# Tile 1's gates moved from the first stage into the gathers, routing at turns 1, 3, 5 and 8, and the first unit's norm, scores and route taken in parts

## The reference, cut to what matters

```python
h = modulate(rms_norm(x, g_mix), sh1, sc1)
q_sb, k_sb, v_sb, q_d, k_d, v_d, gate_sb, gate_d = split(h @ w_in)
merged = sigmoid(gate_sb) * br_sb + sigmoid(gate_d) * br_d
x  = x + gt1 * (merged @ w_out)
h2 = modulate(rms_norm(x, g_ffn), sh2, sc2)
# peer_ffn: for each token and each of 8 heads
q   = h2 @ w_pq                       # two halves of 128
sub = q . keys                        # 2 x 128 scores
s_top, i_top = top_k(sub, 16)         # of each half
best, pos = top_k(s_top[0][:, None] + s_top[1][None, :], 16)
expert = (i_top[0] * 128 + i_top[1])[pos]          # 16 rows per token and head
act = gelu(h2 . peer_u[expert])
out = sum(softmax(best) * act * peer_v[expert])
```

## Time and profile before

| what | value |
|---|---|
| median of 3 runs | 1521.73 us (1521.61 to 1535.05) |
| the profiled execution's own time | 1517.63 us |
| its span | 1515.8 us |
| PE, DVE, ACT, POOL busy | 1319.8, 725.9, 303.8, 557.4 us |
| mean DMA rate | 335 GB/s, 507.33 MB in packets |
| first gather issued | 277.88 us |
| first dots of units 0, 1, 4 and 8 | 282.20, 319.6, 457.67, 665.1 us |

### The profile page before, as it was taken

The page is one execution under the profiler, slowest core; times in us unless marked ns, Lnnn a source line. Parts: engine busy times, 40 slices in busy tenths (PEclk is TensorE's granted clock), DMA queues, the critical chain, the costliest instruction groups (busy, mean ns, idle before and its releaser), DMA issues.

```text
span 1515.8 us, 13732 instructions
## 1 busy us (share of the span) xinstructions
PE 1319.8 (87%) x4628; PEld 746.7 (49%) x4628; DVE 725.9 (48%) x1642; ACT 303.8 (20%) x735; POOL 557.4 (37%) x531
## 2 busy tenths in 40 slices
PE   7999999568779796695798999888898998999997
PEld 7767788434445463342443444343333343554443
DVE  5125333787676566665566575664534322320001
ACT  2221112332211112211221321111110122411102
POOL 1000000477776666676565554645554000000000
PEclk6999999779999898897899999999999999999999
DMA  8945544789999999999999999999999789678882
GB/s 352 399 181 208 205 157 139 259 308 389 385 377 385 409 393 404 409 400 360 370 382 410 409 409 409 409 409 409 409 409 408 276 305 412 225 251 278 286 302 90
DMA packets 135284, 507.33 MB, mean 335 GB/s; under 512 B 15408, under 2 KB 16304, under 8 KB 133168
## 3 DMA queue, kind: packets, MB, share of 16 engines
q0 software_dynamic: 75456, 293.63, 49.4%
q1 hardware_dynamic: 58320, 208.63, 37.5%
q10 hardware_dynamic: 1440, 4.19, 0.7%
HBM read 505.35 MB, written 1.05 MB: 334 GB/s over the span
## 4 chain that ended last, share of the span: by engine, by line
PE 54%; DMA 23%; DVE 8%; another core or an unknown queue 5%; issue 5%; POOL 2%; ACT 2%; SPq 0%; DVEq 0%; ACTq 0%
PE ps_M L844 19%; DMA arena<-in_peer_u,arena 18%; PE ps_M L400 8%; PE ps_T L646 7%; PE ps_T L647 6%; DMA ring<-in_w_second 3%; DVE tmp L1879 3%; PE ps_M L621 2%; PE ps_M L592 2%; PE ps_M L410 2%; DMA ring<-in_peer_v,arena 2%; POOL ring L1113 1%; PE ps_S L421 1%; POOL arena L1100 1%
## 5 line engine op out<-in xcount | busy, mean ns | idle before, releaser
L844 PE MATMUL ps_M<-ring,arena 128*128 128x512 f32 x1088 | 498.5, 601 | 13.1 <-DMA ring<-in_w_second 9.5
L1100 POOL DMA_INDIRECT arena<-in_peer_u,arena x256 | 273.1, 1067 | 267.7 <-DVE tmp L1879 120.8
L1113 POOL DMA_INDIRECT ring<-in_peer_v,arena x256 | 277.1, 1082 | 166.1 <-issue 66.8
L646 PE MATMUL ps_T<-ring,arena 128*128 128x512 f32 x436 | 240.5, 635 | 105.9 <-ACT arena L1251 40.7
L844 PEld LDWEIGHTS ps_M<-ring,arena 128*128 128x128 f32 x1088 | 203.7, 193 | 252.5 <-issue 241.1
L647 PE MATMUL ps_T<-ring,arena 128*128 128x512 f32 x436 | 235.0, 622 | 0.0
L1879 DVE SCALAR_TENSOR_TENSOR tmp<-arena,merged 128x1024 f32<-128x1024 f32 x128 | 156.7, 1224 | 160.6 <-DMA arena<-in_peer_u,arena 135.5
L1879 DVE SCALAR_TENSOR_TENSOR tmp<-arena 128x1024 f32<-128x1024 f32 x128 | 156.6, 1224 | 74.9 <-DMA arena<-in_peer_u,arena 65.9
L646 PEld LDWEIGHTS ps_T<-ring,arena 128*128 128x128 f32 x436 | 77.5, 198 | 200.8 <-issue 143.9
L647 PEld LDWEIGHTS ps_T<-ring,arena 128*128 128x128 f32 x436 | 87.2, 200 | 112.0 <-issue 112.0
L400 PE MATMUL ps_M<-hT,ring 128*128 128x256 f32 x576 | 130.3, 386 | 1.3 <-ACT hT L1264 1.3
(11 more groups left out here) (257 smaller groups left out, 1075.7 us busy)
## 6 DMA issues: line engine op xcount, KB each, us to landing
ring<-in_w_second SPq DMA_DIRECT2D x276, 512.0 KB, 4.5
arena<-in_w_ada POOLq DMA_DIRECT2D x12, 2048.0 KB, 11.0
ring<-in_w_in SPq DMA_DIRECT2D x46, 512.0 KB, 11.4
ring<-in_w_pq SPq DMA_DIRECT2D x32, 512.0 KB
ring<-in_w_out SPq DMA_DIRECT2D x16, 512.0 KB, 4.2
ring<-in_w_br SPq DMA_DIRECT2D x16, 384.0 KB, 3.0
arena<-in_peer_u,arena POOLq DMA_INDIRECT x256
ring<-in_peer_v,arena POOLq DMA_INDIRECT x256
```

The lines of the kernel that those rows point to most:

```text
L646: low = mm(twin[:, 0:512], dg[:, i % 8, :], v_ring[n % VR][:, 0:512], start=first, stop=last)
L844: m = mm(bank, left[c], w[:, c, :], start=first and c == 0, stop=last and c == 1)
L1100: pool.indirect_dma_start(u_ring[:, n % UR, :], None, A["peer_u"][0], bass.IndirectOffsetOnAxis(ap=expert[:, u % 3, k:k + 1], axis=0))\
L1113: pool.indirect_dma_start(v_ring[n % VR], None, A["peer_v"][0], bass.IndirectOffsetOnAxis(ap=expert[:, u % 3, k:k + 1], axis=0))\
```

## The change

Six edits, all in the order of the programs:

1. The gates of tile 1 leave the first stage. `tile_gate(0, ...)` computes tile 0's with 128 moving columns; tile 1's are 16 products `lga`, `lgb`, four in each of phases -1, 0, 1 and 2, at turns 1, 4, 9 and 12 on TensorE and one turn later on ScalarE. SP loads their weights a second time, in `FIRST` between the queries.
2. The route of a unit is at turns 1, 3, 5 and 8 of its phase, where it was at 2, 5, 8 and 11.
3. The sum of squares of unit 0's norm is taken in parts between the products of `out1`.
4. Unit 0's scores are two products in two banks, each behind its own query half, and each half is copied and routed by itself.
5. `stick_scores1(0)`, `stick_old(0)` and `stick_mask1(0)` come later: behind the row transposes on TensorE, behind the row copies on ScalarE, behind unit 0's route on VectorE.
6. `merge` waits for the gate's Tanh by a semaphore of its own.

```diff
+def late_gates(phase):
+    return [(("lga", "lgb")[n % 2], n // 2) for n in range(4 * (phase + 1), 4 * (phase + 2))]
...
+    elif phase < 3:
+        FIRST += late_gates(phase)[:2] + [(f"q{u}", 0), (f"q{u}", 1)] + late_gates(phase)[2:]
...
+            def tile_gate(t, name):
+                bank = claim_m(name)
+                w = tile(name)
+                for c in range(KC):
+                    m = mm(bank[:, 0:P], w[:, c, :], hT[:, c, tile_tok(t)], start=c == 0, stop=c == KC - 1)
+                finish(m, name)
...
+            def norm_part(c):
+                pe.wait_ge(sq_ready, KC + c + 1)
+                m = mm(ps["SA"][:, 0:P], ones[:, :], squares[:, c, :], start=c == 0, stop=c == KC - 1)
+                if c == KC - 1:
+                    finish(m, ("norm2", 0))
...
+            def half_scores(half):
+                name = ("sub", 0, half)
+                bank = claim(("OT", "T0")[half], name)
+                pe.wait_ge(*emptied(("q0", half)))
+                finish(mm(bank[:, 0:NK], qT[:, half, :], keysT[:, half, :], start=True, stop=True), name)
...
-                both_tiles(("ga", c))
-                both_tiles(("gb", c))
+                tile_gate(0, ("ga", c))
+                tile_gate(0, ("gb", c))
...
-            stick_scores1(0)
             for k in range(KC):
                 out1(0, k)
-            tile_norm("SA", ("norm2", 0), 1)
+                if k == 1:
+                    claim("SA", ("norm2", 0))
+                if k > 0:
+                    norm_part(k - 1)
+            norm_part(KC - 1)
             for half in range(2):
                 query(0, half)
-            scores(0)
+                half_scores(half)
             for half in range(2):
                 turn_rows(0, half, f"T{half}")
+            stick_scores1(0)
...
+                if phase < 3 and k in (1, 4, 9, 12):
+                    tile_gate(1, late_gates(phase)[(1, 4, 9, 12).index(k)])
...
-            score_take(0)
+                copy(("sub", 0, half), sub[:, 0, half, :], NK)
...
+                if phase < 3 and k in (2, 5, 10, 13):
+                    name = late_gates(phase)[(2, 5, 10, 13).index(k)]
+                    gate_tile(1, ("lga", "lgb").index(name[0]), name[1], name)
...
+                dve.wait_ge(*emptied((("gb", "lgb")[t], c)))
...
-                    if k in (2, 5):
-                        route_half(u, (k - 2) // 3)
+                    if k in (1, 3):
+                        route_half(u, k // 3)
+                    elif k == 5:
+                        route_best(u)
                     elif k == 8:
-                        route_best(u)
-                    elif k == 11:
                         route_index(u)
```

More of the change, by code:

```diff
@@ L1023, in source @@
                     return w_in_v[:, 24 + n, :]
-                if what in ("ga", "gb"):
-                    return w_in_v[:, 30 + KC * ("ga", "gb").index(what) + n, :]
+                if what[-2:] in ("ga", "gb"):
+                    return w_in_v[:, 30 + KC * ("ga", "gb").index(what[-2:]) + n, :]
                 if what in ("br0", "br1"):
@@ L1251, in diagonal, with gate_tile @@
                 F(dg[:, i % 8, :], ident[:, :], ACT.Copy, scale=wgt[:, u % 2, k:k + 1]).then_inc(diag_ready, 1)
+            def gate_tile(t, s, c, name):
+                act.wait_ge(*produced(name))
+                F(gate[:, t * KC + c, s, :], ps[use[name][0]][:, 0:P], ACT.Tanh, scale=0.5).then_inc(released(name), 1)
             act.wait_ge(vec_in, 16)
@@ L1305, in _ @@
                 for s, name in enumerate((("ga", c), ("gb", c))):
-                    act.wait_ge(*produced(name))
-                    F(gate[:, c:c + KC + 1:KC, s, :], ps[use[name][0]][:, 0:T].rearrange("p (t n) -> p t n", n=P),
-                      ACT.Tanh, scale=0.5).then_inc(released(name), 1)
+                    gate_tile(0, s, c, name)
                 if c == 1:
@@ L1318, in _ @@
                     dil_take(0, 1)
-            stick_old(0)
             F(warm[:, 1:2], eps, ACT.Sqrt)
@@ L1327, in _ @@
                 query_take(0, half)
-            score_take(0)
+                copy(("sub", 0, half), sub[:, 0, half, :], NK)
             for half in range(2):
                 copy(("rows", 0, half), h_rows[0][:, half * 512:(half + 1) * 512], 512)
+            stick_old(0)
             for half in range(2):
@@ L1828, in route_half @@
             def route_half(u, half):
-                if half == 0:
+                if u == 0:
+                    dve.wait_ge(*emptied(("sub", 0, half)))
+                elif half == 0:
                     dve.wait_ge(*emptied(("sub", u)))
@@ L1961, in _ @@
                 merge(0, c)
-            stick_mask1(0)
             own()
@@ L1970, in _ @@
             route_index(0)
+            stick_mask1(0)
             def beside(phase, k):
```

## The result

Over 19 runs of each the changed kernel has a median of 1511.64 us (1498.87 to 1519.12) and the kernel before 1525.21 us (1517.95 to 1535.05): ratio 0.990, 95% interval 0.988 to 0.992. In the rounds of the experiments, where both kernels are faster (before near 1502 us), the changed kernel stood at 0.9933, interval 0.991 to 0.995. The forecast was 1504.6 against 1521.7, 0.989, with a range of 1494 to 1519: a step of 17.1 us, where 13.6 were measured here and 10.3 in the rounds of the experiments.

The account below looks back on a forecast made before the run. TensorE was taken to bound the first stage and DMA bytes at 409 GB/s the gather stage. First gather 26.1 us earlier, gather stage 9.0 us longer: -17.1 us, giving 1504.6 us, range 1494 to 1519.

Parts of the forecast that it names:

- Three stages, the second bound by its bytes: Whole kernel: TensorE bounds the first stage, DMA bytes at 409 GB/s the gather stage; the last moves unchanged.
- Gates, 23.8 us: First stage: 16 gate tiles each lose 1.70 us, 27.2 together, less 3.4 lost waiting for a modulation chunk.
- The wait for chunk 9: TensorE in the first stage's gates: waits 4.4 us for this modulation chunk instead of 0.97, losing 3.4 us of gain.
- Chunk 11 and the ring's loads: First stage's modulation and weight loads: in time, the chunk with 0.4 us of room; if late, 5 to 8 us less gain.
- Attention scores 2.0, norm -0.9: Before the first gather: scores leave TensorE's path, gaining 2.0 us; unit 0's norm in parts loses 0.9.
- Scores and route, 1.2: Unit 0 before the first gather: scoring and routing each half by itself gains 1.2 us.
- The bytes, 20.5 less 8.5 less 3: Gather stage: second load costs 20.5 us at 409 GB/s; unit 0's room returns 8.5, units 1 to 3 return 3.
- Earlier indices, 2 us and the 1.4 MB of rows in unit 0, 3.4 us: Gather stage: POOL waits less for route indices, gaining 2 us later and bringing 1.4 MB of rows forward in unit 0.
- TensorE's lag, 2 us: Gather stage, phases 0 to 2: added gate products delay rows and ScalarE, costing 2 us, bounds 0 and 8.
- The slower rival: Phases 0 to 2: TensorE becomes the bound at the halved clock, +22.9 us, 1545; chance 0.05.
- The rival of bytes paid in full: Gather stage: the second load gets no free room, so -5.6 us in all, 1516; band 1511 to 1525, chance 0.28.
- the one in which the room takes nearly all: Gather stage: units 0 to 3 fill to 409 GB/s and index waits vanish, -26 us, 1496; chance 0.12.

Follow-up runs that it names:

- no_second_load: The changed kernel without the second load of the 16 gate tiles, tile 1's gates computed with the keys as weights; 0.9839 of the kernel before, median 1477.01 us.
- one_product: The changed kernel with only the first of the eight products of each of tile 1's gate tiles, all loads kept; 0.9941 of the kernel before.
- busy_wait: The changed kernel with one gate tile's eight products issued three times over, filling TensorE's wait for modulation chunk 9; 0.9932 of the kernel before.
- changed_again: The changed kernel unaltered, run again on one chip with the kernel before for a second trace; 0.9933 of the kernel before, median 1492.14 us.
- gates_only: The kernel before with only the move of tile 1's gates beside the gathers (edits to gates and merge's semaphore); 0.9934 of the kernel before.
- route_only: The kernel before with only the route of a unit moved to turns 1, 3, 5 and 8; 0.9994 of the kernel before.
- chunk9_later: The changed kernel with TensorE's sums of modulation chunk 9 one column tile later, behind the gates of c = 3; 0.9921 of the kernel before.

## Why the prediction was right, point by point

- **Three stages, the second bound by its bytes.** Right, and more strictly than the prediction used it: with a granted clock of 0.96 to 0.99 the stage is its bytes over 409 GB/s plus what room unit 0 leaves. Taking bytes away won 15.1 us (no_second_load), taking products away nothing (one_product). Of the Trainium skill's page "DMA: Bandwidth & Descriptors", the rule that loads from all queues share one set of DMA engines ("Issuing engines are not separate DMA queues") is borne out here, by SP's tiles that cost the rows 15.1 us; the figure of 358 GB/s ("Where 436 GB/s comes from") is not, the stage runs at 409.
- **Gates, 23.8 us.** 62.5 us became 40.7 to 41.8: 20.7 to 21.8. The wait for chunk 9 was 4.20 us, where 4.4 were predicted. Not in the sum was what it does to the clock, 3.4 to 6.8 us at the lower level, worth 1.6 us by busy_wait; with the clock whole the gates take 39.1 us, and 38.7 was the sum. Chunk 11 and the ring's loads were in time.
- **Attention scores 2.0, norm -0.9.** Measured 12.8 to 10.7 us between the first branch product and `out1`, and 16.4 to 17.2 us from there to the root: a gain of 2.1 and a loss of 0.8.
- **Scores and route, 1.2.** The working holds where the clock is alike: with 3.4 us of halved clock 18.2 to 18.5 us from the root to the first gather, against 19.0 to 20.1 in the kernels whose scores are in one piece (in changed_again a gain of 1.6). But the clock goes down around these queries, at a wait of 2.79 us that all kernels have: in the kernels in one piece for 3.4 us at most (not at all in the first trace of before), in those in parts for 3.4 us in half of the ten traces and 6.8 in the others. So in the first pair there is a loss of 1.5. The first gather in all: 24.8 us earlier, predicted 26.1.
- **The bytes, 20.5 less 8.5 less 3.** This is the term that was mis-sized. The gather stage, from the first gather to the last dot, grew by 15.9 us where the sum had 9.0, and of the 20.5 us 15.1 were paid. The step that failed is the room that unit 0 was said to give, 8.5 us: by the two traces of one chip it gave 13.9 - 9.7 = 4.2. Its rate was to rise to 370 GB/s or more and rose to 324 in the one trace of the changed kernel and 328 in the other. Of the 8.5, 3.4 were rows that the earlier indices were to bring (next point). And the loads were not free there: two query tiles and a gate tile go out from 3 us ahead of the first gather to 1.4 us behind it, and the first dot comes 7.8 us behind the first gather instead of 4.4. Without the gate tiles it is 5.4 (no_second_load), and with them but without the other parts of the change 4.2 (gates_only), so it takes both; that it is these three tiles that stand before the first row was read from the times and not tested alone. Units 1 to 3 grew by 10.5 us, as the prediction's sign had it, and gave what was taken and a little more, 4.2 us where the sum has 3, although their room was smaller than the 9.1 of the first trace: at a clock of 0.99 instead of 0.92 the kernel before runs there at 395 GB/s, and the room is 134.3 x (1 - 395/409) = 4.6 us.
- **Earlier indices, 2 us and the 1.4 MB of rows in unit 0, 3.4 us.** Wrong: route_only is 0.9994. POOL's wait for indices was removed there, and the stage from the first gather to the last dot stayed as long.
- **TensorE's lag, 2 us.** Nothing, by one_product. One sign that the prediction named did appear in the first trace of the changed kernel: VectorE waited 18.3 us in tile 1's `merge` and not 13.4, but the stretch was no longer than its bytes. The slower rival, 1545, is out.

The number held because the first stage gave nearly what it should and the range was wide enough for the rest. In the traces of one chip it is -24.8 + 15.9 = -8.9 us at the last dot, and 10.3 us between the medians of that group; the sum had -17.1. In the 19 runs of the result 13.6 us lie between the medians; their trace of before has more room (36 us from the first dot on, 28 after) at a lower granted clock. That the clock is the reason is argued from the traces and was not tested. The sum knows nothing of it, so that the runs of the result came nearer to the sum than those of the experiments is in part luck. The rival of bytes paid in full was close: as a step 13.6 us is nearer to 17.1 than to its 5.6, but the measured 1511.64 is nearer to its 1516 than to 1504.6 and lies at the lower edge of the band, 1511 to 1525, that it was given, and in the rounds of the experiments the step of 10.3 is nearer to 5.6. The truth lay between the two. The slower rival and the one in which the room takes nearly all did not come.

## What to carry to other kernels

In a stage whose DMA rate is flat, price a change by the bytes that it adds, at that rate, and what adds no bytes at nothing: waits of the issuing engine, added products and earlier indices had no price here, and 8.39 MB had 15 us. Work that is moved behind a stage border to save 1.70 us and needs a second load of 1.28 us wins little once the stage has no room, so move the first few and stop; eight tiles did as much as sixteen. A step that is won ahead of the first gather counts only if the first row comes earlier too: 3.7 us of it were 0.1 at the first dot. And a tighter schedule makes waits where none was seen before: order TensorE's work so that it has something to do in them.

## What the runs showed that I had not expected

- A wait of 4.20 us of TensorE is followed by 3.4 to 6.8 us at the halved clock, in each of the five traces that have the wait; with 3.6 us of it filled there was none. A wait of 1.73 us, in chunk9_later, had 3.4 us of it behind it as well.
- The same program shows such stretches at different places from one execution to the next (81 and 143 us in some traces and not in others). Over all traces the first gate product lies between 166.5 and 171.8 us, so two single profiles could not have told this change from none: 2.0 us lie between them and 13.6 between the medians.
- The kernel before ran at a median near 1502 us in the groups of the experiments and at 1525 in the runs of the result, and the change's ratio differed with it, 0.9933 and 0.990.
